# Output-step weights of an expert layer in 2 MB transfers into three slots, the third being the slot of the one-hot matrices

## The reference

```
s = (x @ w_query) . sub_keys ; top 16 of 128 x 128 experts for each of 8 heads ; gate = softmax
a = down[idx] . x            # a dot product with each chosen expert's row
c = gate * gelu(a)
y = sum over the 8 x 16 choices of c * up[idx]
```

## Time and profile before

| | us |
|---|---|
| median of 3 runs | 2564.48 (2564.28 to 2564.83) |
| the profiled execution's own time | 2567.89 |
| its span | 2566.1 |
| TensorE busy | 2449.9 (95%) |
| output steps begin in the first layer | 542.88 |
| fold begins, first and second layer | 855.53 and 1713.03 |

### The profile page before, as it was taken

One profiled execution on the slowest core, in us unless ns is written; L12 is line 12 of the kernel. 1 busy time (PEld: TensorE's weight loads), 2 busy tenths in 40 slices (PEclk: granted clock), 3 DMA queues, 4 the chain that ended last, 5 costly groups with the idle time before them and its releaser, 6 DMA issues.

```text
span 2566.1 us, 36447 instructions
## 1 busy us (share of the span) xinstructions
PE 2449.9 (95%) x14770; PEld 2032.4 (79%) x14770; DVE 1247.5 (49%) x2710; ACT 523.2 (20%) x1700; POOL 230.1 (9%) x256
## 2 busy tenths in 40 slices
PE   8999999998988999999999998889999999999998
PEld 7558999998888765699999888878566687876665
DVE  5734979964444385198798444445300010541001
ACT  2121235520111112022454111112000001420000
POOL 0000122121111000012212111100000000000000
PEclk9999999999999999999999999999999999879999
DMA  6303899999999522269999999983244442003443
GB/s 219 127 38 139 329 392 418 398 413 421 421 421 420 211 105 93 82 234 412 395 404 405 421 421 421 421 337 131 99 154 157 147 164 99 1 1 131 148 148 114
DMA packets 88105, 642.18 MB, mean 250 GB/s; under 512 B 11739, under 2 KB 14274, under 8 KB 15502
## 3 DMA queue, kind: packets, MB, share of 16 engines
q1 hardware_dynamic: 55596, 420.85, 41.9%
q0 software_dynamic: 31360, 218.33, 20.7%
q10 hardware_dynamic: 994, 0.82, 0.1%
HBM read 638.69 MB, written 1.06 MB: 249 GB/s over the span
## 4 chain that ended last, share of the span: by engine, by line
PE 78%; DMA 18%; DVE 3%; ACT 1%; issue 1%; SPq 0%; DVEq 0%; ACTq 0%
PE bank L786 20%; DMA weight_ring<-in_experts 18%; PE bank L538 9%; PE bank L552 9%; PE bank L560 9%; PE bank L808 7%; PE bank L503 4%; PE bank L515 3%; PE bank L797 3%; PE bank L911 2%; PE bank L465 1%; PE bank L469 1%; PE bank L960 1%; PE bank L527 1%; PE bank L979 1%; DVE hidden_T L1367 1%
## 5 line engine op out<-in xcount | busy, mean ns | idle before, releaser
L808 PE MATMUL bank<-arena,weight_ring 128*128 128x152 f32 x4096 | 555.8, 295 | 61.9 <-DMA weight_ring<-in_experts 61.9
L808 PEld LDWEIGHTS bank<-arena,weight_ring 128*128 128x128 f32 x4096 | 533.3, 190 | 85.3 <-issue 43.9
L786 PE MATMUL bank<-hidden_T,weight_ring 128*128 128x152 f32 x4096 | 544.1, 293 | 1.2 <-DMA weight_ring<-in_experts 1.2
L786 PEld LDWEIGHTS bank<-hidden_T,weight_ring 128*128 128x128 f32 x4096 | 532.9, 190 | 2.8 <-DMA weight_ring<-in_experts 2.3
L1662 DVE CUSTOM_DVE_ANT_0 arena<-arena 128x1024 f32<-128x1024 f32 x208 | 254.4, 1223 | 325.2 <-DMA arena<-in_expert_rows,choice_by_pair 324.8
L1026 POOL DMA_INDIRECT arena<-in_expert_rows,choice_by_pair x208 | 203.3, 977 | 864.7 <-DVE arena L1675 822.8
L1675 DVE SCALAR_TENSOR_TENSOR arena<-arena,pair_weights 128x1024 f32<-128x1024 f32 x202 | 258.7, 1281 | 21.7 <-ACT pair_weights L1180 21.2
L538 PE MATMUL bank<-hidden_T,weight_ring 128*128 128x256 f32 (+1 forms) x1088 | 240.5, 381 | 7.9 <-DVE hidden_T L1367 7.6
L552 PEld LDWEIGHTS bank<-hidden_T,weight_ring 128*128 128x128 f32 x1024 | 194.4, 190 | 55.0 <-issue 28.7
L538 PEld LDWEIGHTS bank<-hidden_T,weight_ring 128*128 128x128 f32 (+1 forms) x1088 | 201.5, 187 | 41.6 <-DVE hidden_T L1367 9.0
L552 PE MATMUL bank<-hidden_T,weight_ring 128*128 128x256 f32 x1024 | 231.3, 379 | 2.5 <-DVE hidden_T L1367 2.5
(11 more groups left out here) (340 smaller groups left out, 2086.3 us busy)
## 6 DMA issues: line engine op xcount, KB each, us to landing
weight_ring<-in_experts SPq DMA_DIRECT2D x256, 1024.0 KB
weight_ring<-in_mlp SPq DMA_DIRECT2D x64, 1024.0 KB
weight_ring<-in_dense_h SPq DMA_DIRECT2D x22, 2048.0 KB, 7.6
weight_ring<-in_dense_nsa SPq DMA_DIRECT2D x9, 2048.0 KB, 7.8
weight_ring<-in_dense_rg SPq DMA_DIRECT2D x7, 2048.0 KB, 7.7
arena<-in_expert_rows,choice_by_pair POOLq DMA_INDIRECT x208
arena<-distance_bias_scratch SPq DMA_DIRECT2D x2, 768.0 KB, 6.1
residual<-in_x SPq DMA_DIRECT2D x1, 1024.0 KB, 5.5
```

The source lines that it names most:

```text
L786: last = mm(bank[s % 3][:, 0:DT_TOK], w[:, k * P:(k + 1) * P], HT[:, k, 0:DT_TOK], start=k == 0, stop=k == KD - 1)
L808: last = mm(bank[4 + k // 2][:, (k % 2) * DT_TOK:(k % 2 + 1) * DT_TOK], w[:, k * P:(k + 1) * P], HACT[:, s, :], start=s == 0 and k % 2 == ...
```

## The change

The up weights get an array of their own, with four steps (2 MB) to a transfer, so that a partition's row is 16 KB. There are 32 of them in place of 64 transfers (`BACKS`). They go to the slots 0, 1 and 2 in turn (`back_slot`); slot 2, with the one-hot matrices, is used from the third transfer on, once `gated` and `late_gated` say that the last gates are made. Each slot has its semaphore. The first two transfers wait for the last pair of steps in their slot (`hidden_ready` >= 124 and 128), later ones for `step_used`, which now counts fours of steps. The next section's first block goes to slot 2 as before, but waits for `step_used` >= 30 too. The transfers of the down weights, and the arithmetic, stay.

```diff
-    pairs = lambda v: ...
-    m["experts"] = np.concatenate([pairs(down), pairs(up)], 1)
+    m["experts_down"] = by_steps(down, 2)
+    m["experts_up"] = by_steps(up, 4)
...
+def back_slot(layer, d):
+    return ((layer % 2, 1 - layer % 2, 2))[d % SLOTS]
+back_loaded = ("step_loaded0", "step_loaded2", "step_loaded1")
...
-                for i in range(PAIRS):
+                for i in range(PAIRS // 2):
...
+                for d in range(BACKS):
+                    s = back_slot(l, d)
+                    if d < 2:
+                        sp.wait_ge(S["hidden_ready"], NKEYS - 4 + 4 * d)
+                    elif d == 2:
+                        sp.wait_ge(S["gated"], GROUPS)
+                        sp.wait_ge(S["late_gated"], NKEYS - 1 - CUT[0])
                     else:
-                        sp.wait_ge(S["step_used"], i - RING + 1 - PAIRS // 2)
+                        sp.wait_ge(S["step_used"], d - 2)
+                    sp.dma_start(ring[:, s * SLOT:(s + 1) * SLOT], load_back(d)).then_inc(S[back_loaded[back_slot(l, d)]], 16)
...
-                sp.wait_ge(S["late_gated"], NKEYS - 1 - CUT[0])
                 sp.wait_ge(S["pair_added"], TILES - GBUF)
                 for b in range(SLOTS):
-                    if b:
-                        sp.wait_ge(S["step_used"], PAIRS // 2 - 4 + 2 * b)
+                    sp.wait_ge(S["step_used"], BACKS - 2 + b)
                     block(l + 1, b, ahead)
...
                 def back(s):
-                    i = NKEYS // 2 + s // 2
-                    r = buffer_of(l, i)
-                    pe.wait_ge(S[f"step_loaded{r}"], 16 * (i // RING + 1))
-                    w = ring[:, r * 2048 + (s % 2) * 1024:r * 2048 + (s % 2 + 1) * 1024]
+                    d = s // 4
+                    pe.wait_ge(S[back_loaded[back_slot(l, d)]], 16 * (PAIRS // 2 // RING + d // SLOTS + 1))
+                    at = back_slot(l, d) * SLOT + (s % 4) * 1024
+                    w = ring[:, at:at + 1024]
...
-                    if s % 2:
+                    if s % 4 == 3:
                         last.then_inc(S["step_used"], 1)
```

More of the change, by code:

```diff
@@ L65 @@
 PAIRS = NKEYS
+BACKS = NKEYS // 4
 SECTION_BLOCKS = (HYBRID_BLOCKS, HYBRID_BLOCKS, RG_BLOCKS_N, NSA_BLOCKS)
@@ L380, in stream, with peer @@
                         block(n + 1, b, ahead)
-            def peer(l, load, ahead):
+            def peer(l, load, load_back, ahead):
                 last_in_slot = {slot_of(l, b): b for b in range(HYBRID_BLOCKS)}
-                for i in range(PAIRS):
+                for i in range(PAIRS // 2):
                     r = buffer_of(l, i)
@@ L389, in peer @@
                         sp.wait_ge(S["proj_done"], 2 * last_in_slot[r // 2] + 2)
-                    elif i < PAIRS // 2 + RING:
+                    else:
                         sp.wait_ge(S["hidden_ready"], 2 * (i - RING + 1))
-                    else:
-                        sp.wait_ge(S["step_used"], i - RING + 1 - PAIRS // 2)
-                    sp.dma_start(ring[:, r * 2048:(r + 1) * 2048], load(i)).then_inc(S[f"step_loaded{r}"], 16)
-                    if i == PAIRS // 2 + 16:
+                    sp.dma_start(ring[:, r * 2048:(r + 1) * 2048], load(i)).then_inc(S[f"step_loaded{r}"], 16)
+                for d in range(BACKS):
[5 more added lines that the diff above has]
+                        sp.wait_ge(S["late_gated"], NKEYS - 1 - CUT[0])
+                    else:
+                        sp.wait_ge(S["step_used"], d - 2)
+                    sp.dma_start(ring[:, s * SLOT:(s + 1) * SLOT], load_back(d)).then_inc(S[back_loaded[back_slot(l, d)]], 16)
+                    if d == 8:
                         sp.wait_ge(S["hidden_kept"], kept(NKEYS - 1))
-                        sp.wait_ge(S["gated"], GROUPS)
                         clear(front_names[:len(front_names) // 2])
-                    if i == PAIRS // 2 + 20:
+                    if d == 10:
                         clear(front_names[len(front_names) // 2:])
-                sp.wait_ge(S["late_gated"], NKEYS - 1 - CUT[0])
                 sp.wait_ge(S["pair_added"], TILES - GBUF)
                 for b in range(SLOTS):
-                    if b:
-                        sp.wait_ge(S["step_used"], PAIRS // 2 - 4 + 2 * b)
+                    sp.wait_ge(S["step_used"], BACKS - 2 + b)
                     block(l + 1, b, ahead)
@@ L434, in _ @@
             dense(0, hybrid_block[0])
-            peer(0, lambda i: I["experts"][0, i], hybrid_block[1])
+            peer(0, lambda i: I["experts_down"][0, i], lambda d: I["experts_up"][0, d], hybrid_block[1])
             section_clear(0, stream_names + peer_names)
@@ L438, in _ @@
             dense(1, hybrid_block[1])
-            peer(1, lambda i: I["experts"][1, i], rg_block)
+            peer(1, lambda i: I["experts_down"][1, i], lambda d: I["experts_up"][1, d], rg_block)
             section_clear(1, stream_names)
@@ L845, in peer @@
                         last.then_inc(S["pair_rows"], 1)
-                pe.wait_ge(S["step_used"], PAIRS // 2)
+                pe.wait_ge(S["step_used"], BACKS)
                 pe.sem_inc(S["down_done"], 1)
@@ L2094, in layouts @@
     up = a["peer_up"].reshape(DEPTH, NKEYS, NKEYS, D).transpose(0, 2, 1, 3)
-    pairs = lambda v: v.reshape(DEPTH, NKEYS // 2, 2, P, D).transpose(0, 1, 3, 2, 4).reshape(DEPTH, NKEYS // 2, P, 2 * D)
-    m["experts"] = np.concatenate([pairs(down), pairs(up)], 1)
+    by_steps = lambda v, n: v.reshape(DEPTH, NKEYS // n, n, P, D).transpose(0, 1, 3, 2, 4).reshape(DEPTH, NKEYS // n, P, n * D)
+    m["experts_down"] = by_steps(down, 2)
+    m["experts_up"] = by_steps(up, 4)
     m["expert_rows"] = np.concatenate([a["peer_down"].reshape(-1, D), a["peer_up"].reshape(-1, D)], 1)
```

## The result

The changed kernel takes 2599.45 us (median of 4 runs, 2594.74 to 2602.7) against 2564.65 before: a ratio of 1.0127, with a 95% interval of 1.0114 to 1.014. It is 34.8 us slower. The forecast was 2580 with a range of 2554 to 2590, so the direction was right and the forecast change, 15 us, was less than half of what came. The traced execution of the changed kernel took 2594.74, the shortest of the four; its span is 2592.9 against 2566.1, 26.8 us more. The ratios of this document leave out one execution, of the kernel that follows the tiles: it took 5225.61 us, twice as long as that kernel's other four, for a reason that is not known.

What follows compares the result with a forecast made beforehand. The prediction took DMA bytes to bound the output-step stage, with TensorE only waiting its turn. Per layer +4.2 (fold) and +3.4 (clock) made +7.6, twice +15.2, on 2564.5: 2580 us, range 2554 to 2590.

Steps and rivals of the forecast that it cites:

- Bound by bytes, and shares by rows: Output-step stage: DMA bytes bound it at 421 GB/s; 16 KB weight rows beside 8 KB gather rows get two thirds.
- The two thirds: Weights' share of the DMA engines beside gathers in the output steps, q1 near 250 GB/s and q0 near 171.
- The output steps: TensorE starts near 543, runs almost without weight waits (31.0 us gone), and ends its steps near 825, 30 us earlier.
- The pause: At step 72 TensorE waits 10 us for ScalarE, resuming at 708.5; costs nothing as long as gathers end later.
- Gathers alone: Stretches 705 to 717 and 809 to the end, some 19 tiles at 2.7 us each: +3.9 us a layer.
- The blocks' collision: Layer's end: next section's three blocks delay tile 103, its dot 14.8 us after dot(100): +6.7 us, bounds 0 and +8.
- The clock: Fold and part of the transposes run at 1.2 GHz after TensorE idles some 35 us: +3.4 us a layer, bounds 0 and +5.5.
- The sum: Per layer, fold +4.2 and clock +3.4 give +7.6 us; twice for both layers, +15.2.
- No collision: Rival at the layer's end: all as forecast but the blocks' 6.7; +0.9 us a layer, 2566 (2562 to 2569), chance 0.18.
- faster tail: Rival at the layer's end: gathers keep 2.5 us a tile, blocks cost nothing, clock holds; -6.4 us a layer, 2552, chance 0.14.

Runs made afterwards that it cites:

- the kernel that follows the tiles: Changed kernel with next section's blocks at pair_added >= 104, plus two unused matmuls after each of the last 18 tiles' additions: 2580.75 us, ratio 1.0054.
- The 8 KB kernel: Changed kernel with the same three slots and 2 MB transfers, each moved as 256 rows of 8 KB instead of 128 of 16 KB: 2571.13 us, ratio 1.0025.
- step 72's experiment: Changed kernel with the matmul that waits for ScalarE placed after output step 82 instead of 72: 2597.02 us, ratio 1.0127.
- the kernel with gathers alone: Changed kernel with only the first three of a layer's 32 up-weight transfers, leaving out work the result needs: 2485.68 us.
- the first experiment: Changed kernel with SyncE loading the next section's three blocks at pair_added >= 104 instead of 100: 2585.03 us, ratio 1.0068.
- M = 4: Changed kernel with blocks at pair_added >= 104, 16 KB rows in a layer's first 4 up-weight transfers, 8 KB in the other 28: 2559.99 us, ratio 0.9983.

## Why the prediction was right in direction and wrong in size

- **Bound by bytes, and shares by rows: right.** 424 GB/s against 421 before; 256 and 168 GB/s against 250 and 171 forecast. The 8 KB kernel shows that the row size is the cause. The two thirds show in most windows of 2 us, as in the first two lines (600 to 602 us). In every fourth such window q0 leads, as in the last two (606 to 608 us), and over longer stretches it is 1.5 to one. TensorE uses up 2 MB in 8.4 us, as the forecast had it, so q1 should run out of work once in that time; that it does is inferred and not seen directly.

```profile
q1 hardware_dynamic: 36, 0.57, 67.5%
q0 software_dynamic: 38, 0.26, 31.5%
...
q0 software_dynamic: 75, 0.57, 67.4%
q1 hardware_dynamic: 33, 0.28, 33.3%
```

- **The output steps: right.** TensorE began at 544.28 (forecast 543), paused 6.8 us before L860 (10), resumed at 706.57 (708.5), ended at 826.5 (825). The pause was free, as step 72's experiment shows.
- **Gathers alone: wrong, and this is the step that failed.** The forecast took 2.7 us a tile, "bounds: VectorE's 2.51 a tile and 2.9". They ran at 3.2 us in the first layer (dot(88) at 811.11, dot(100) at 849.65), which is 6.1 us more than forecast on twelve tiles. Dot(88) itself was some 2.5 us late; the other stretch with gathers alone follows the pause at step 72, and from 712 to 717 the engines moved only 147 GB/s. Together dot(100) came at 849.65 instead of near 841, 8.6 us late. In the second layer the pace was 3.0 us, and dot(100) came 6.2 us later than the same sum gives. The term was mis-sized in one place: for issue to landing I took 2.49 + 2.6 from SyncE's lone 2 MB block; a gather with two others in flight took 7.2 us here (811 to 850) and 7.3 in the kernel with gathers alone. The trace of before had a nearer row that I passed over because weights loaded beside it: the layer's first gather, issued at 289.74, had its dot at 297.97, 8.2 us. It would have given (2.7 + 8.2) / 3 = 3.6 as the upper bound. The forecast's 2.7 us a tile is 388 GB/s, more than gathers alone moved in any stretch above. The nearer row, from the timelines of GpSimd and VectorE before:

```profile
289.74 1.02 POOL L1026 DMA_INDIRECT arena<-in_expert_rows,choice_by_pair  x1 [5.76 <-DMA choice_by_pair<-choice_pack]
...
297.97 1.23 DVE L1662 CUSTOM_DVE_ANT_0 arena<-arena 128x1024 f32<-128x1024 f32 x1 [3.78 <-DMA arena<-in_expert_rows,choice_by_pair]
```

- **The blocks' collision: right.** Dot(103) came 15.7 us after dot(100), and 15.3 in the second layer, forecast 14.8; the first experiment removed about 5 us of it.
- **The clock: right in kind, its size by luck.** From fold to section's end it was +3.4 us in the first layer, as forecast, and +1.8 in the second. Part of that is not the clock: TensorE's wait for SyncE before L485 was 4.06 us instead of 3.61 in the first layer and 2.42 instead of 2.89 in the second. The tracking matmuls gave back 2.7 in both.
- **The sum.** Forecast +4.2 and +3.4 a layer; measured +13.7 and +3.4 in the first, +10.8 and +1.8 in the second, and -3 behind them. For the traced execution the forecast was 2583.1 and 2594.74 came: 9.5 us more in the first layer, of which the gathers are 8.6, and 5.1 in the second, less those 3. To double the first layer's 8.6 + 0.9 would give 2599, the median, but the second layer was not like the first, so that agreement is luck. Where the other 8 us of the median come from no trace shows.
- **The rivals.** "No collision" and "faster tail" both needed gathers that keep the engines full by themselves. They don't (318 to 329 GB/s), so the lower part of the range, from 2554 up, had nothing under it.

## What to carry to other kernels

When two streams share full DMA engines, a larger row on one takes time from the other and adds none. First ask which stream ends the stage, then set the row sizes so that both end together; here that was worth 0.17%. A stream that ran beside another may not be able to fill the engines alone: before counting on it to catch up, add up its buffer loop (use, release, issue, landing) over the tiles in flight, with an issue-to-landing time from that same kind of transfer.

## What was not expected of the hardware

- Two queues with 8 KB rows each moved 3636 and 3641 packets in 130 us. With 16 KB rows on one of them the packets were about even in most windows of 2 us (36 and 38 from 600 to 602) and the bytes went two to one (0.57 and 0.26 MB). A packet of these views is one row; how many rows an engine takes from a queue in one turn they do not show.
- Gathers alone held an engine 0.33 us for a packet, beside the weights 0.28, and so moved 318 GB/s at a DMA share of 0.90.
- TensorE's clock fell to half after a pause of 2.1 us that followed 38 us of back-to-back matmuls. In the tracked kernel a pause of 2.0 us did the same: 0.50 from 860 to 862, back at 1.00 before the fold began at 866.06. Pauses of 1.1 and 1.9 us before the two folds with M = 4, and of 0.6 to 0.9 in the second layer of the tracked kernel, left the folds at full rate. These runs do not settle which pause is too long.
- GpSimd's issue of a gather took 1.7 to 2.0 us in place of 0.94 for some of the tiles that came in quick succession (for instance at 817.52 in the changed kernel); its cause is open.
